# One written-out sequence for the heads of the mLSTM and differential attentions

## Chip, cores and metric

One core of one Trainium2 chip runs the whole program in a single launch. The metric is the device time of that launch in microseconds, the median of several runs.

## What is computed

The reference passes 256 tokens of width 1024 through a first block of two layers and a second block of two layers. Each layer of the first block is a mixer, an attention to a memory of 256 tokens, and a convolutional feed-forward part; the second block has a feed-forward part, a hybrid mixer, an attention to a second memory, and another feed-forward part. Two of the mixers hold an attention with *two* sets of scores for each of four heads, each head with values of width 128:

```python
# layer 0: mLSTM, forward and backward in time (bwd is the same on flipped inputs)
sc  = einsum('bhtd,bhsd->bhts', qc, kc) * exp(log_d - m_t)      # log_d from the gates, causal
h   = (sc @ v) / maximum(abs(sum(sc)), exp(-m_t))               # fwd + bwd are added
# layer 1: differential attention
p   = softmax(q1 @ k1.T + bias) - lam * softmax(q2 @ k2.T + bias)
out = p @ v
...
# everything around them is matrix products in float32
x = x + mixer(...) ; x = x + cross_attention(x, mem) ; x = x + conv_ffn(x)
```

## The kernel before, in words

**Products in float32.** Each float32 factor is kept as two parts of reduced precision (a rounded `hi` and the rest `lo`), and a product is three matmuls, x_hi·w_lo, x_lo·w_hi and x_hi·w_hi, summed in one PSUM bank (lines 882, 883 and 885). Weights arrive in chunks of 128x2048 numbers. A chunk's way is: a DMA by SyncE into one of three `raw` buffers (line 760), the rounded part by ScalarE (`whi`, line 1398), and the subtraction raw − whi either by VectorE as one instruction (`wlo`, line 1843) or by GpSimd as four (line 850). There are three buffers of `whi` and `wlo`, so rounding chunk c waits until TensorE has used chunk c − 3, and a new DMA waits until the chunk three before it has been subtracted. A list made while the program is built says which engine subtracts: chunks whose units are first used as fillers of an attention or heads stage go to GpSimd if that stage was built after `on_pool` was set (its field `late`).

**Units and fillers.** A unit is one accumulation of two 128x256 results, held in one of two banks; a bank is free again when its result has been copied out, by ScalarE for units called "plain" (line 1416), else by VectorE (lines 1861, 1870 and 1874). Attention and "heads" (normalisation) stages have small matmuls that wait for other engines, so units of later linear layers are put between them: `fill` is a table from a slot to (the unit up to which TensorE goes, the unit up to which the others copy out, and optionally how many chunks ahead they prepare). Slot "pre" lies at the barrier between two stages, where every engine drains and then waits for the two others. TensorE does the slot's units before that wait, ScalarE and VectorE do theirs behind it.

**The fillers here.** In the mLSTM stage: H0 and H1 (two half-length residual units of the output weights, from one chunk), then K0 to K3 (keys and values of the memory, one chunk each, behind a chunk that holds the memory's activations). H2 and H3, from one chunk, come in the heads stage behind it. In the differential stage: K3, then H0, H1, H2; H3 comes behind it.

**The two stages.** Both are built by `attention(...)` and carried out by three functions called `dual`, one in the program of each engine. One head i is:

- TensorE: `scores(i)` (line 1236, for the mLSTM also line 1249), `turn(i)` (four transposes, line 1260), `values(i)` (line 1269).
- VectorE: `front(i)` (biased scores and their extremes, line 2147, and 2305), `prob(i)` (for the mLSTM line 2323 on; scaling in lines 2334 and 2337), `output(i)` (line 2343).
- ScalarE: `front(i)` (exponentials, line 1710), `back(i)` (copies the transposed probabilities, line 1721).

The score banks of two heads exist, so `scores(i)` waits for `prob(i-2)`; the transposes share one bank, and so do the results of `values`. Before the change each engine ran a loop over i with a fixed distance `lag` of 2 between the first and the last step of a head:

```python
# TensorE                          # ScalarE                        # VectorE
scores(i)                          # empty_and_fill(st, i)          # empty(st, i); front(i)
fill(st, i)                        # front(i)                       # fill(st, i)
turn(i - lag)                      # back(i - lag)                  # prob(i - 1)
values(i - lag - 1)                # (tanh at i == 6)               # output(i - lag - 1)
```

`empty` copies out units up to the slot's second number, `split_upto(reach(st, slot))` prepares chunks. Each engine works through its program in order, so whatever stands in front of a step holds it up.

## Time and profile before

| | us |
|---|---|
| median of 3 runs | 2294.79 |
| lowest and highest | 2292.48, 2295.53 |
| the profiled execution's own time | 2294.97 |
| its span in the profile | 2293.2 |
| TensorE busy in it | 2203.7 (96%) |
| VectorE, ScalarE, GpSimd busy | 1504.9, 1108.0, 355.9 |
| chain that ended last, TensorE's share | 85% |
| the mLSTM stage in it | about 133 to 186 us |
| the differential stage in it | about 572 to 606 us |

The span is what the profiler saw from first to last instruction; the execution's own time is 1.8 us longer. Times in rows are counted from the span's start. A row of a timeline is the start, the time taken, engine, line, instruction, and in brackets how long the engine had been idle before it and what ended that idleness. `x4` says that four instructions are merged in the row.

### The profile page before, as it was taken

The numbers are of one execution on the slowest core, as the hardware profiler recorded it, in microseconds if no ns is written. First come the engines' busy times: TensorE is split into PE (matmuls) and PEld (weight loads), VectorE is DVE, ScalarE is ACT, GpSimd is POOL, SyncE is SP. The second block draws the span as 40 slices with busy tenths as digits, with TensorE's granted clock in tenths as the row PEclk, the third lists the DMA queues.
The fourth block names the chain that finished last, engine by engine and source line by source line (L and its number), as shares of the span: only waits on it lengthen the run. The fifth ranks groups of instructions, "written<-read, shape, count | busy, mean of one in ns | idle before, by whom it ended". The sixth has DMA issues, their size and how long they took to land.

```text
span 2293.2 us, 40427 instructions
## 1 busy us (share of the span) xinstructions
PE 2203.7 (96%) x17458; PEld 2112.2 (92%) x17458; DVE 1504.9 (66%) x2210; ACT 1108.0 (48%) x1335; POOL 355.9 (16%) x300
## 2 busy tenths in 40 slices
PE   8988999998799999999999999999999999999998
PEld 7777899997689999999988799999999998799998
DVE  6656787843578787567766657657656566657655
ACT  5345654544465445335646455335334456455333
POOL 2760000055000000000645120000000015320000
PEclk9989999999999999999999999999999999999999
DMA  8653355543245555546643354555555653355552
GB/s 280 181 165 111 111 188 198 176 158 117 92 131 168 200 174 189 189 166 184 195 143 104 124 182 163 195 176 184 184 184 167 175 166 105 117 171 169 185 184 92
DMA packets 316964, 375.13 MB, mean 164 GB/s; under 512 B 27255, under 2 KB 283011, under 8 KB 315635
## 3 DMA queue, kind: packets, MB, share of 16 engines
q1 hardware_dynamic: 311635, 354.88, 47.4%
q0 software_dynamic: 3424, 11.50, 1.8%
q10 hardware_dynamic: 1728, 6.17, 0.7%
q8 instruction: 138, 2.26, 0.4%
q14 instruction: 39, 0.32, 0.0%
HBM read 363.34 MB, written 9.18 MB: 162 GB/s over the span
## 4 chain that ended last, share of the span: by engine, by line
PE 85%; DVE 7%; ACT 3%; issue 2%; DMA 1%; SPq 1%; DVEq 0%; POOL 0%; ACTq 0%
PE banks L882 24%; PE banks L885 23%; PE banks L883 23%; PE banks L923 3%; PE banks L924 3%; PE banks L927 3%; DVE wlo L1843 2%; PE banks L1147 1%; DMA raw<-in_ev_w_in 1%; PE banks L1185 1%; ACT whi L1398 1%; PE banks L1171 1%; PE banks L1045 1%; SPq L760 1%; PE banks L892 0%
## 5 line engine op out<-in xcount | busy, mean ns | idle before, releaser
L882 PE MATMUL banks<-x_hi,wlo 128*128 128x256 f32 (+1 forms) x4344 | 1101.5, 286 | 18.2 <-DVE gt L1879 6.9
L883 PE MATMUL banks<-x_lo,whi 128*128 128x256 f32 (+1 forms) x4344 | 1092.3, 284 | 0.0
L1398 ACT ACTIVATE whi<-raw 128x2048 fp32r<-128x2048 f32 (+3 forms) x340 | 637.7, 1879 | 601.1 <-PE banks L885 551.8
L882 PEld LDWEIGHTS banks<-x_hi,wlo 128*128 128x128 f32 (+1 forms) x4344 | 838.4, 193 | 37.0 <-issue 19.8
L883 PEld LDWEIGHTS banks<-x_lo,whi 128*128 128x128 f32 (+1 forms) x4344 | 839.0, 193 | 0.0
L1843 DVE TENSOR_TENSOR wlo<-raw,whi 128x2048 fp32r<-128x2048 f32 (+4 forms) x290 | 652.3, 2260 | 120.6 <-ACT whi L1398 120.3
L885 PE MATMUL banks<-x_hi,whi 128*128 128x256 f32 x4344 | 687.9, 284 | 0.0
L885 PEld LDWEIGHTS banks<-x_hi,whi 128*128 128x128 f32 x4344 | 595.8, 193 | 3.2
L850 POOL TENSOR_TENSOR wlo<-raw,whi 128x512 fp32r<-128x512 f32 x192 | 251.7, 1347 | 1121.4 <-ACT whi L1398 1121.4
L923 PE MATMUL banks<-x_hi,wlo 128*128 128x256 f32 (+1 forms) x624 | 170.5, 305 | 13.9 <-DVE gt L1879 5.0
L924 PE MATMUL banks<-x_lo,whi 128*128 128x256 f32 (+1 forms) x624 | 163.9, 295 | 0.0
L923 PEld LDWEIGHTS banks<-x_hi,wlo 128*128 128x128 f32 (+1 forms) x624 | 127.6, 204 | 20.8 <-issue 6.1
L2409 DVE TENSOR_TENSOR wk<-banks,norm_scale 128x512 f32<-128x512 f32 x132 | 90.9, 689 | 74.2 <-PE banks L885 69.6
L924 PEld LDWEIGHTS banks<-x_lo,whi 128*128 128x128 f32 (+1 forms) x624 | 127.7, 205 | 0.4
L805 POOL TENSOR_SCALAR gt<-gt,cols 128x256 f32<-128x256 f32 x32 | 42.6, 1343 | 544.8 <-DVE gt L1921 544.8
L2448 DVE CAST x_hi<-wk 128x512 fp32r<-128x512 f32 x66 | 28.2, 427 | 131.6 <-PE banks L885 130.6
L2427 DVE SCALAR_TENSOR_TENSOR wk<-wk,cols 128x255 f32<-128x255 f32 x176 | 73.4, 480 | 39.4 <-ACT wk L1763 38.7
L882 PE MATMUL banks<-whi,x_lo 128*128 128x256 f32 (+3 forms) x400 | 96.7, 282 | 0.0
L883 PE MATMUL banks<-wlo,x_hi 128*128 128x256 f32 (+3 forms) x400 | 95.3, 279 | 0.0
L927 PE MATMUL banks<-x_hi,whi 128*128 128x256 f32 (+1 forms) x632 | 92.9, 285 | 0.0
L1763 ACT ACTIVATE wk<-wk,cols 128x256 f32<-128x256 f32 x88 | 45.7, 590 | 92.0 <-DVE wk L2409 92.0
L1447 ACT ACTIVATE x_hi<-xT,con,cols 128x256 fp32r<-128x256 f32 x112 | 60.9, 590 | 59.7 <-DVE xT L1874 49.8
(264 smaller groups left out, 1939.0 us busy)
## 6 DMA issues: line engine op xcount, KB each, us to landing
raw<-in_ffn_w_gu SPq DMA_DIRECT2D x88, 1024.0 KB, 5.1
raw<-in_ffn_w_down SPq DMA_DIRECT2D x66, 1024.0 KB, 5.2
raw<-in_ffn_w_up SPq DMA_DIRECT2D x44, 1024.0 KB, 5.1
raw<-in_w_in SPq DMA_DIRECT2D x38, 1024.0 KB, 5.2
raw<-in_ca_w_kv SPq DMA_DIRECT2D x16, 1024.0 KB, 5.3
raw<-in_od_w_in SPq DMA_DIRECT2D x12, 1024.0 KB, 5.3
raw<-in_ev_w_in SPq DMA_DIRECT2D x10, 1024.0 KB, 7.4
raw<-in_ca_w_q SPq DMA_DIRECT2D x8, 1024.0 KB, 5.1
```

The source lines that it names most:

```text
L850: m = eng.tensor_tensor(wlo[s][:, at:at + PIECE], full[:, at:at + PIECE], whi[s][:, at:at + PIECE].bitcast(F32), ALU.subtract)
L882: eng.matmul(out, a[1], b[0], start=first and i == 0, stop=False, skip_group_check=True)
L883: eng.matmul(out, a[0], b[1], start=False, stop=False, skip_group_check=True)
L885: m = eng.matmul(out, a[0], b[0], start=False, stop=last and i == len(operands) - 1, skip_group_check=True)
L923: eng.matmul(bank[:, o], a[1], b[0], start=i == 0 and k0 + k == 0, stop=False, skip_group_check=True)
L924: eng.matmul(bank[:, o], a[0], b[1], start=False, stop=False, skip_group_check=True)
L927: m = eng.matmul(bank[:, o], a[0], b[0], start=False, stop=k == n - 1, skip_group_check=True)
L1398: eng.activation(whi[s % SETS][:, 0:ch["n"]], raw[i % SLOTS][:, 0:ch["n"]], ACT.Copy).then_inc(S["weights_hi"], 1)
L1447: eng.activation(X[nm["buf"]][0][:, k, :], xT[:, k, :], ACT.Identity, scale=cols[:, nm["gain"] + k:nm["gain"] + k + 1], bias=C("zero")).th ...
L1843: eng.tensor_tensor(wlo[s][:, 0:n], full[:, 0:n], whi[s][:, 0:n].bitcast(F32), ALU.subtract).then_inc(S["weights_split"], 1)
L2409: return eng.tensor_tensor(wk[:, half, :].rearrange("p (n c) -> p n c", c=SEQ), bank[:, :].rearrange("p (n c) -> p n c", c=SEQ), norms, AL ...
L2427: m = eng.scalar_tensor_tensor(out=o, in0=wk[:, half, i * SEQ:(i + 1) * SEQ][:, src], scalar=cols[:, w:w + 1], in1=o, op0=ALU.mult, op1=AL ...
```

## The change

In both stages the loop over i gives way to a sequence written out step by step, in one agreed order for the three engines. Both first scores come ahead of all fillers. On TensorE `turn(i)` comes right behind `scores(i+2)`. ScalarE takes both first fronts before rounding further chunks, and no longer rounds two chunks ahead in a row before a front. VectorE takes `prob` ahead of chunk subtractions. In the differential stage slot 0 prepares one chunk ahead and no more.

In the mLSTM stage the chunk of K0 is now rounded at the barrier ("pre", 3 chunks ahead). `on_pool` is set after that stage instead of before it, so of this stage's chunks only K0's stays with GpSimd; the chunks of H0/H1, K1, K2 and K3 are subtracted by VectorE.

```diff
@@ even_mixer
-            on_pool[0] = True
+            chunks[units_of[K[0]]["chunk"]]["on_pool"] = True
             attention("mlstm", [...],
-                      fill={"pre": (M[7] + 1, M[7] + 1, 2), 0: (H[1] + 1, M[7] + 1, 2), 1: (K[1], K[0]), 2: (K[2], K[1]), 3: (K[3], K[2]), 4: (K[3] + 1, K[3])},
-                      tanh={6: M[7] + 1})
+                      fill={"pre": (M[7] + 1, M[7] + 1, 3), 0: (H[1] + 1, H[1], 3), 1: (K[1], K[0]), 2: (K[2], K[0]), 3: (K[3], K[2]), 4: (K[3] + 1, K[3])},
+                      tanh=M[7] + 1)
+            on_pool[0] = True
@@ odd_mixer
             attention("difference", [...],
-                      fill={0: (H[1], K[3]), 1: (H[2], H[1]), 2: (H[3], H[2])})
+                      fill={0: (H[1], K[3], 1), 1: (H[2], H[1]), 2: (H[3], H[2])})
@@ tensor, dual
-                for i in range(len(units) + lag + 1):
-                    if i < len(units):
-                        scores(i)
-                    fill(st, i)
-                    if 0 <= i - lag < len(units):
-                        turn(i - lag)
-                    if i - lag >= 1:
-                        values(i - lag - 1)
+                scores(0)
+                scores(1)
+                fill(st, 0)
+                if kind == "mlstm":
+                    fill(st, 1)
+                scores(2)
+                turn(0)
+                scores(3)
+                if kind == "mlstm":
+                    values(0)
+                    turn(1)
+                    fill(st, 2)
+                    values(1)
+                    turn(2)
+                    fill(st, 3)
+                    values(2)
+                    turn(3)
+                    fill(st, 4)
+                    values(3)
+                else:
+                    fill(st, 1)
+                    turn(1)
+                    values(0)
+                    fill(st, 2)
+                    values(1)
+                    turn(2)
+                    values(2)
+                    turn(3)
+                    values(3)
@@ scalar, dual
+                if kind == "mlstm":
+                    front(0)
+                    front(1)
+                    round_ahead(st, 0)
+                    evac_upto(st["fill"][1][0])
+                    round_ahead(st, 1)
+                    back(0)
+                    back(1)
+                    front(2)
+                    front(3)
+                    empty(st, 3)
+                    round_ahead(st, 2)
+                    back(2)
+                    empty(st, 4)
+                    round_ahead(st, 3)
+                    back(3)
+                    round_ahead(st, 4)
+                    flush(st["tanh"])
+                else:
+                    empty(st, 0)
+                    round_ahead(st, 0)
+                    front(0)
+                    front(1)
+                    empty(st, 1)
+                    round_ahead(st, 1)
+                    back(0)
+                    front(2)
+                    front(3)
+                    back(1)
+                    round_ahead(st, 2)
+                    back(2)
+                    back(3)
@@ vector, dual
+                front(0)
+                front(1)
+                if kind == "mlstm":
+                    empty(st, 0)
+                    prob(0)
+                    empty(st, 1)
+                    prob(1)
+                    split_upto(reach(st, 0))
+                    front(2)
+                    front(3)
+                    split_upto(reach(st, 1))
+                    output(0)
+                    prob(2)
+                    prob(3)
+                    output(1)
+                    split_upto(reach(st, 2))
+                    output(2)
+                    split_upto(reach(st, 3))
+                    output(3)
+                    split_upto(reach(st, 4))
+                else:
+                    prob(0)
+                    prob(1)
+                    empty(st, 1)
+                    front(2)
+                    front(3)
+                    prob(2)
+                    output(0)
+                    prob(3)
+                    empty(st, 2)
+                    output(1)
+                    split_upto(reach(st, 1))
+                    output(2)
+                    split_upto(reach(st, 2))
+                    output(3)
```

**How the instructions move.** ScalarE in the mLSTM stage. `x_hi<-raw` is the memory's chunk, `whi<-raw` a rounded weight chunk, `wk<-wk,stat` the exponentials of a front, `ft<-banks` the copy-out of K0, `wk<-banks` a `back`. Before:

```order
L1391 ACTIVATE x_hi<-raw 128x2048
L1398 ACTIVATE whi<-raw 128x2048
L1710 ACTIVATE wk<-wk,stat 128x256 x4
L1713 ACTIVATE stat<-stat 128x4
L1398 ACTIVATE whi<-raw 128x2048 x2
L1710 ACTIVATE wk<-wk,stat 128x256 x4
L1713 ACTIVATE stat<-stat 128x4
L1416 ACTIVATE ft<-banks 128x512
L1398 ACTIVATE whi<-raw 128x2048
L1710 ACTIVATE wk<-wk,stat 128x256 x4
```

With the change:

```order
L1413 ACTIVATE x_hi<-raw 128x2048
L1420 ACTIVATE whi<-raw 128x2048
L1734 ACTIVATE wk<-wk,stat 128x256 x4
L1737 ACTIVATE stat<-stat 128x4
L1734 ACTIVATE wk<-wk,stat 128x256 x4
L1737 ACTIVATE stat<-stat 128x4
L1420 ACTIVATE whi<-raw 128x2048
L1438 ACTIVATE ft<-banks 128x512
L1420 ACTIVATE whi<-raw 128x2048
L1745 ACTIVATE wk<-banks 128x512 x2
```

The exponentials of head 1 no longer have two roundings in front of them; the two first `back` steps stand together behind the chunk of K2.

TensorE in the mLSTM stage, behind K0 (`banks<-x_hi,whi` is the end of its product). Before, this place holds one pair of scores and then the next filler:

```order
L885 MATMUL banks<-x_hi,whi 128x256 x8
L1236 MATMUL banks<-ft 128x256 x2
L1249 MATMUL banks<-gate_rows_parts,pick 128x512
L882 MATMUL banks<-x_hi,wlo 128x256
L883 MATMUL banks<-x_lo,whi 128x256
```

With the change two heads' scores, two turns and one `values` stand there:

```order
L886 MATMUL banks<-x_hi,whi 128x256 x8
L1237 MATMUL banks<-ft 128x256 x2
L1250 MATMUL banks<-gate_rows_parts,pick 128x512
L1261 MATMUL banks<-con,wk 128x128 x4
L1237 MATMUL banks<-ft 128x256 x2
L1250 MATMUL banks<-gate_rows_parts,pick 128x512
L1270 MATMUL banks<-wk,vt 128x256 x2
L1261 MATMUL banks<-con,wk 128x128 x4
L883 MATMUL banks<-x_hi,wlo 128x256
```

ScalarE in the differential stage (`vt<-banks` copies out K2, then K3). Before:

```order
L1416 ACTIVATE vt<-banks 128x2x256
L1398 ACTIVATE whi<-raw 128x2048 x2
L1710 ACTIVATE wk,stat<-wk,stat 128x256 x4
L1416 ACTIVATE vt<-banks 128x2x256
L1710 ACTIVATE wk,stat<-wk,stat 128x256 x4
L1398 ACTIVATE whi<-raw 128x2048
```

With the change:

```order
L1438 ACTIVATE vt<-banks 128x2x256
L1420 ACTIVATE whi<-raw 128x2048
L1734 ACTIVATE wk,stat<-wk,stat 128x256 x8
L1438 ACTIVATE vt<-banks 128x2x256
L1420 ACTIVATE whi<-raw 128x2048
L1745 ACTIVATE wk<-banks 128x512
```

One rounding of the two stands behind both first fronts and behind the copy-out of K3.

## Rows read from the trace of the kernel before

**Rows 1.** The page: busy time of each engine over the whole span.

```profile
PE 2203.7 (96%) x17458; PEld 2112.2 (92%) x17458; DVE 1504.9 (66%) x2210; ACT 1108.0 (48%) x1335; POOL 355.9 (16%) x300
```

**Rows 2.** The stretches' busy PE, PEld, DVE, ACT, POOL; PEclk, DMA share, GB/s.

```profile
133.00:186.00 53.00, 45.48 (x292) 40.09 (x292) 37.17 (x105) 26.07 (x37) 25.82 (x20) 0.87 0.44 150
572.00:606.00 34.00, 26.89 (x186) 23.03 (x184) 19.89 (x63) 16.97 (x41) 6.01 (x5) 0.95 0.39 129
```

**Rows 3.** Waits between 132 and 190 us: engine, line <- awaited: total us, times, longest.

```profile
PE banks L1236 <- DVE wk L2337: 5.8, 1, 5.8
PE banks L1260 <- DVE wk L2337: 0.9, 1, 0.9
PE banks L1269 <- DVE ft L2343: 0.6, 1, 0.6
```

**Rows 4.** VectorE's timeline, first and last rows of `prob(0)`, then of `prob(1)`.

```profile
147.16 0.41 DVE L2323 CUSTOM_DVE_ANT_0 wk<-banks,wk 128x256 f32<-128x256 f32 x1
153.66 2.77 DVE L2337 SCALAR_TENSOR_TENSOR wk<-wk,stat 128x256 f32<-128x256 f32 x2
...
160.90 0.42 DVE L2323 CUSTOM_DVE_ANT_0 wk<-banks,wk 128x256 f32<-128x256 f32 x1
163.65 0.88 DVE L2337 SCALAR_TENSOR_TENSOR wk<-wk,stat 128x256 f32<-128x256 f32 x2
```

**Rows 5.** GpSimd's timeline, 132 to 172 us.

```profile
136.77 5.44 POOL L850 TENSOR_TENSOR wlo<-raw,whi 128x512 fp32r<-128x512 f32 x4 [6.66 <-ACT whi L1398]
143.44 15.33 POOL L850 TENSOR_TENSOR wlo<-raw,whi 128x512 fp32r<-128x512 f32 x12 [1.23 <-ACT whi L1398]
```

**Rows 6.** TensorE around its longest wait, ScalarE behind K0, the stretch after the wait.

```profile
143.32 1.03 PE L1236 MATMUL banks<-ft 128*128 128x256 f32 x4
...
150.76 0.60 ACT L1416 ACTIVATE ft<-banks 128x512 f32<-128x512 f32 x1 [1.68 <-PE banks L885]
...
156.49 2.07 PE L1236 MATMUL banks<-ft 128*128 128x256 f32 x4 [5.77 <-DVE wk L2337]
...
156.00:160.00 4.00, 3.51 (x8) 2.25 (x9) 1.11 (x4) 0.00 (x0) 2.77 (x3) 0.50 0.51 194
```

**Rows 7.** Timelines at the first stage's end: VectorE, ScalarE, TensorE.

```profile
176.71 2.29 DVE L1843 TENSOR_TENSOR wlo<-raw,whi 128x2048 fp32r<-128x2048 f32 x1 [0.92 <-ACT whi L1398]
...
186.60 1.91 ACT L1398 ACTIVATE whi<-raw 128x2048 fp32r<-128x2048 f32 x1 [0.24 <-DVEq L1817]
...
189.45 0.81 PE L1045 MATMUL banks<-wk,con 128*8 128x256 f32 x3 [0.24 <-ACT wk L1578]
```

**Rows 8.** Waits between 572 and 610 us.

```profile
ACT whi L1398 <- PE banks L885: 4.9, 1, 4.9
PE banks L1260 <- ACT wk L1721: 2.8, 1, 2.8
PE banks L1236 <- DVE wk L2337: 2.8, 2, 2.2
PE banks L882 <- ACT vt L1416: 0.7, 1, 0.7
```

**Rows 9.** The second stage: ScalarE's first exponentials, TensorE's tail, the clock there.

```profile
581.43 0.49 ACT L1710 ACTIVATE wk<-wk,stat 128x256 f32<-128x256 f32 x1
...
596.20 1.03 PE L1269 MATMUL banks<-wk,vt 128*128 128x256 f32 x4
...
600.51 1.92 PE L1269 MATMUL banks<-wk,vt 128*128 128x256 f32 x4
...
605.16 1.10 PE L1269 MATMUL banks<-wk,vt 128*128 128x256 f32 x4 [0.61 <-DVE ft L2343]
...
600.00:604.00 4.00, 3.97 (x15) 3.30 (x16) 1.85 (x5) 1.19 (x2) 0.00 (x0) 0.57 0.00 0
```

**Rows 10.** Timelines behind the second stage: ScalarE, TensorE.

```profile
606.86 1.34 ACT L1578 ACTIVATE wk<-ft 128x256 f32<-128x256 f32 x4 [2.95 <-DVEq L1817]
...
609.55 1.68 PE L1045 MATMUL banks<-wk,con 128*8 128x256 f32 x7
```

More of the change, by code:

```diff
@@ L464, in attention @@
             alone = all(len(un["heads"]) == 1 for un in units) if not dual else False
-            stage("attention", att=kind, units=units, alone=alone, u0=number("att", len(units)), bufs=2, lag=2,
+            stage("attention", att=kind, units=units, alone=alone, u0=number("att", len(units)), bufs=2,
                   sc=[banks[i] for i in (0, 1, 6, 7)] if dual else bank_pairs[0], pt=[banks[2]] if dual else bank_pairs[1],
@@ L1230, in dual @@
             def dual(st):
-                units, kind, bufs, lag = st["units"], st["att"], st["bufs"], st["lag"]
+                units, kind, bufs = st["units"], st["att"], st["bufs"]
                 sc, pt, ob = st["sc"], st["pt"], st["ob"]
@@ L1422, in fill, with empty, round_ahead @@
                     evac_upto(st["fill"][slot][1])
-            def empty_and_fill(st, slot):
-                if slot in st["fill"]:
-                    evac_upto(st["fill"][slot][1])
-                    split_upto(reach(st, slot))
+            def empty(st, slot):
+                evac_upto(st["fill"][slot][1])
+            def round_ahead(st, slot):
+                split_upto(reach(st, slot))
             gated = [0]
@@ L1701, in dual @@
             def dual(st):
-                units, kind, bufs, lag, pt = st["units"], st["att"], st["bufs"], st["lag"], st["pt"]
+                units, kind, bufs, pt = st["units"], st["att"], st["bufs"], st["pt"]
                 def front(i):
@@ L1721, in back @@
                     eng.activation(probsT_flat[b], pt[0], ACT.Copy).then_inc(S["att_pts"], 1)
-                for i in range(len(units) + lag + 1):
-                    if i < len(units) + lag:
-                        empty_and_fill(st, i)
-                    if i < len(units):
-                        front(i)
-                    if lag <= i < len(units) + lag:
-                        back(i - lag)
-                    if i in st.get("tanh", {}):
-                        flush(st["tanh"][i])
+                if kind == "mlstm":
[30 more added lines that the diff above has]
+                    back(3)
             def index(st):
@@ L2282, in dual @@
             def dual(st):
-                units, kind, bufs, lag = st["units"], st["att"], st["bufs"], st["lag"]
+                units, kind, bufs = st["units"], st["att"], st["bufs"]
                 sc, ob = st["sc"], st["ob"]
@@ L2343, in output @@
                     eng.tensor_copy(units[i]["dst"], ob[0][:, 0:SEQ]).then_inc(S["att_done"], 1)
-                for i in range(len(units) + lag + 1):
-                    empty(st, i)
-                    if i < len(units):
-                        front(i)
-                    fill(st, i)
-                    if 1 <= i <= len(units):
-                        prob(i - 1)
-                    if i - lag >= 1:
-                        output(i - lag - 1)
+                front(0)
[33 more added lines that the diff above has]
+                    output(3)
             def index(st):
```

## The prediction

> **What bounds the kernel now.** The page comes first: TensorE is busy 96% of the span [rows 1]. So only time in which TensorE stands idle, or runs at its lower clock, can be won by moving instructions. The busy times by stretch then say where that is: in the mLSTM stage TensorE is busy 45.5 of 53 us at a mean granted clock of 0.87, in the differential stage 26.9 of 34 us at 0.95, while no other engine is full in either; VectorE is nearest with 37.2 of 53 us [rows 2]. Outside the two stages the change moves only one subtraction.
>
> Third, the waits. In the first stage TensorE waits once for 5.8 us, for line 2337, the end of `prob(0)`, then 0.9 and 0.6 us at the end [rows 3]. Why is `prob(0)` late? VectorE's timeline has it from 147.16 to 156.43, 9.3 us, and `prob(1)` from 160.90 to 164.53, 3.6 us, for the same instructions; line 2337, for one, takes 1.4 us a piece in the one and 0.44 in the other [rows 4]. GpSimd subtracts weight pieces without a gap from 143.4 to 158.8, over the whole of `prob(0)` and not over `prob(1)` [rows 5]. So GpSimd's work makes it 5.6 us longer, and besides it stands behind `front(1)`. After the wait the granted clock is 0.50 from 156 to 160 (1.2 GHz), and four score matmuls take 2.07 us instead of 1.03 [rows 6].
>
> In the second stage ScalarE stands still 4.9 us in front of a rounding whose buffer TensorE still uses, with the exponentials of head 0 queued behind it. TensorE then waits 0.7 us for a copy-out, 2.8 us in two pieces for `prob`, and 2.8 us for a `back` [rows 8]. It waits 0.6 us more for an `output`, and from 600 to 604 it has a clock of 0.57: a `values` step takes 1.92 us instead of 1.03 [rows 9].
>
> **The change, part by part.** No matmul is added or removed. I count TensorE's lost time in each stage, and then what stays of it.
>
> *mLSTM, what goes.* `prob(0)` is issued behind both fronts and the copy-out of H0, but with H0, H1 and K0 of TensorE's work in front of the `scores(2)` that need it: all that work ends at 150.76 now, where ScalarE copies K0 out [rows 6], and no later in the new order, since it is the same work. Before, `scores(1)` started at 143.32 behind H0 and H1 [rows 6]; now they are done ahead, so the fronts and H0's copy-out are over by some 142. GpSimd then has only K0's four pieces, 5.4 us from 136.8 [rows 5], done by 142.2, just as `prob(0)` starts. At the price of `prob(1)`, 3.6 us [rows 4], it ends near 146, and `prob(1)` near 150. The wait of 5.8 us goes. With it goes the slow clock: 3.5 us busy at half clock [rows 2, 6] cost 1.75 us. The two waits at the end, 0.9 and 0.6 us, stand between `turn` and `values` steps with no filler; now K3 lies between `values(2)` with `turn(3)` and `values(3)`, so they go. Sum: 5.8 + 0.9 + 0.6 + 1.75 = 9.05 us.
>
> *mLSTM, what comes.* VectorE takes over the subtractions of K1, K2 and K3, 2.29 us each by [rows 7]; that of H0/H1 falls into the attention before, where VectorE is waiting. Its busy time goes from 37.2 by +6.9, and by −5.6 for the shorter `prob(0)`: about as before, so it is no bound over the stage. Late next is each chunk: K1's ends near 152.5 and is needed near 155.5, K2's has some 4 us of margin, K3's some 2. Cost nothing; if those margins fail, TensorE waits the difference. The last subtraction (the first chunk of the linear layer to come) moves from the middle of the stage behind `output(3)`, in front of the barrier: +2.29 us for ScalarE, which waits there for VectorE and whose rounding at 186.60 and squares lead to TensorE's sums at 189.45 [rows 7]. TensorE has H2 as cover, about 3 us, and before it had only 0.24 us of wait left there, so I count the 2.29 in full. `values(0)` needs `back(0)`, which stands behind the copy-out of K0 and a rounding (0.6 + 1.9 us behind K0's end [rows 6, 7]), against scores, turn and scores on TensorE, 3.3 us: a close race. I take 0.7 us for it and the longer queues; bounds are 0 and the 1.9 us of a rounding [rows 7]. Net: 9.05 − 2.29 − 0.7 = 6.0 us.
>
> *Differential stage.* ScalarE rounds one chunk, then does both fronts, so the exponentials no longer stand behind a wait of 4.9 us and a rounding of 1.9; they start near 575 instead of 581.43 [rows 8, 9]. K3 and H0 cover both `prob` steps, which need no unit of their stage. The waits of 0.7, 2.8 and 2.8 us [rows 8] and of 0.6 us [rows 9] go, 6.9 in all, and the slow clock, (1 − 0.57) x 3.97 = 1.7 us [rows 9]. Left is the end: behind H2 there are no fillers, and the chain `turn`, `back`, `values` stays for heads 2 and 3, each with about 0.8 us in which TensorE waits for the copy. 8.6 − 1.6 = 7.0; I take 0.4 off for hops between engines: 6.6 us. Behind the stage ScalarE's squares start at 606.86, TensorE's sums at 609.55 without a wait [rows 10], so a stage that ends earlier moves them as a whole; VectorE's two subtractions, now at the end, finish about when TensorE does.
>
> *Other edits.* The earlier rounding of K0's chunk changes nothing on ScalarE: it was already the next instruction there. The subtraction of H0/H1 on VectorE frees a `raw` buffer earlier. Those of the following linear layer free theirs some 8 to 14 us later in the differential stage; the DMAs behind them have the whole heads stage as cover, more than 20 us. I count zero; uncovered, a transfer would cost up to what is gained.
>
> **Sum.** 6.0 + 6.6 = 12.6 us. 2294.97 − 12.6 = 2282.4 for the profiled execution; the median of the runs is 0.2 us lower: 2282.2. The bounds: 0.7 + 0.4 back and the split hidden gives 2278.5; with both stages at half, 2288.5.
>
> The Trainium skill (SBUF — State Buffer, "Who interferes with whom") says that a VectorE instruction with two SBUF inputs, or in a 2-port mode, is fully blocked while a GpSimd instruction holds their common port, and that a VectorE instruction with at most one SBUF input is not. The slow line 2337 has two SBUF inputs and is the longer one beside GpSimd [rows 4], so the trace agrees. By that rule alone each moved subtraction would itself be open to such a block, by up to one GpSimd piece; the sum would change by about 1.3 us, since only K0's four pieces still run in the stage's first part.
>
> **Rivals.**
> 1. *The slow clock stays in the differential tail.* TensorE still has thin work there, heads 2 and 3 without fillers. For it: the clock fell behind a stretch of that kind at 600. Against: two waits of 0.8 us instead of 2.2 and 2.8. Price 1.7 us: 2283.9. The Trainium skill (TensorE: Matmul & The Clock Gate, "What's actually happening") says that the activity of the engine decides its clock; by that rule either outcome is possible here, and the price is that of rows 9. Chance 0.15.
> 2. *Only one stage gains in full.* In the differential tail VectorE's `output(1)`, a 2.3 us subtraction and `output(2)` are in one queue; if `values(3)` waits for `output(2)` behind that subtraction, and TensorE's tail keeps its length, that stage gives 2 us: 2286.8. Chance 0.12.
> 3. *The stall only moves.* `prob(0)` now stands behind the copy-out of H0, and each stage's end behind VectorE's subtractions; or a late DMA of the next layer takes the gain back. Then 2294.8. Against it: `prob(0)` has some 8 us up to K0's end for its 3.6. Chance 0.08.
> 4. *VectorE becomes the bound, and it is slower.* If its `prob` steps stayed at the 9.3 us that `prob(0)` has beside GpSimd, for all four heads, VectorE would need 37.2 + 6.9 + 3 x 5.6 = 61 us in a stage that lasts 53. It decides from the point where VectorE's need passes 53 us, that is from two contended heads on. It gives +8 us, +3.5 for two slow-clock spells as in [rows 6], +3.5 for first scores and last values outside VectorE's part, −6.6 from the other stage: 2303. Against: 12 of the 16 GpSimd pieces in [rows 5] are gone. Chance 0.04.
>
> **Numbers.** My forecast has 0.61: 2282.2, its own range 2278.5 to 2286. A measurement here can tell 0.2%, 4.6 us, so faster means below 2290.2. Forecast and rivals 1 and 2 are faster: 0.61 + 0.15 + 0.12 = 0.88, of which I move 0.02 to "same" for a sum that is too high throughout: 0.86. Same: 0.08 + 0.02 = 0.10. Slower: 0.04. Range: 2278.5 to 2289.5, which leaves out rivals 3 and 4 and the tails.
>
> **What would show it.** In the profile of the changed kernel: no wait of TensorE for line 2384 (the old 2337) above 1 us in the mLSTM stage; `prob(0)` in 3.6 to 4.5 us; GpSimd with four pieces there before 145; a granted clock of 1.0 from about 140 on; TensorE's sums behind the stage near 183.5 instead of 189.5. In the differential stage: exponentials of head 0 near 569 (575 less the 6 us already won), sums near 597 instead of 609.55. POOL busy falls by 16 pieces, about 20 us, and that by itself wins nothing. The prediction is wrong if TensorE waits for a `wlo` of VectorE inside the stages, if VectorE is busy without a gap in the first, or if the gain up to 190 or 610 us is lost again in the next attention.

## The result, and the profile after

| | before | changed |
|---|---|---|
| median of six runs each, us | 2294.76 | 2283.11 |
| lowest and highest | 2292.48, 2295.53 | 2277.11, 2285.82 |
| the profiled execution's own time | 2294.97 | 2277.11 |
| ratio, with its 95% interval | | 0.9948 [0.9934, 0.9962] |

The profiled execution of the changed kernel is its fastest run, 6 us below the median. So the two traces differ by more than the medians do, and the first question is where. The starts of four places, taken from TensorE's timelines (the ends are the spans'):

| us | before | changed | difference |
|---|---|---|---|
| first scores of the mLSTM stage | 133.05 | 131.95 | -1.1 |
| sums behind that stage | 189.45 | 181.02 | -8.4 |
| first scores of the differential stage | 572.43 | 564.08 | -8.4 |
| sums behind that stage | 609.55 | 593.60 | -16.0 |
| end of the span | 2293.2 | 2275.3 | -17.9 |

The mLSTM stage gives 7.3 us (56.40 to 49.07), the differential stage 7.6 us (37.12 to 29.52). Between the two stages nothing is given back in this profile. 1.1 us ahead of the first stage and 1.9 us behind the second lie in code that the change does not touch; the experiments below tell more of both.

The page of the changed kernel answers [rows 1]: TensorE and GpSimd are less busy, VectorE a little more.

```profile
PE 2198.8 (97%) x17458; PEld 2108.5 (93%) x17458; DVE 1507.4 (66%) x2214; ACT 1107.6 (49%) x1335; POOL 336.0 (15%) x284
...
PE 89%; DVE 6%; ACT 3%; issue 1%; DVEq 0%; DMA 0%; ACTq 0%
```

The second line is the chain that ended last: TensorE has 89% of it, where it had 85%. GpSimd lost 19.9 us and 16 pieces; VectorE gained only 2.5 us, since its `prob(0)` alone is 5.6 us shorter.

The waits between 131 and 183 us, of TensorE and what it meets at the stage's end, answer [rows 3]:

```profile
DVE ft L2390 <- PE banks L1270: 7.9, 2, 6.6
...
ACT whi L1420 <- DVEq L1864: 3.5, 1, 3.5
...
PE banks L1046 <- ACT wk L1602: 2.3, 1, 2.3
...
PE banks L1237 <- DVEq L1864: 1.1, 1, 1.1
```

TensorE's 5.8, 0.9 and 0.6 us are gone. What is left is the 1.1 us at the barrier in front of the stage, which was there before, and a new one of 2.3 us for the squares behind the stage. VectorE's timeline shows `prob(0)` and `prob(1)`, first and last rows, then the first chunk's subtraction; it answers [rows 4]:

```profile
141.76 0.42 DVE L2370 CUSTOM_DVE_ANT_0 wk<-banks,wk 128x256 f32<-128x256 f32 x1
...
144.51 0.88 DVE L2384 SCALAR_TENSOR_TENSOR wk<-wk,stat 128x256 f32<-128x256 f32 x2
...
145.91 0.41 DVE L2370 CUSTOM_DVE_ANT_0 wk<-banks,wk 128x256 f32<-128x256 f32 x1
...
148.66 0.88 DVE L2384 SCALAR_TENSOR_TENSOR wk<-wk,stat 128x256 f32<-128x256 f32 x2
149.47 2.28 DVE L1890 TENSOR_TENSOR wlo<-raw,whi 128x2048 fp32r<-128x2048 f32 x1
```

`prob(0)` takes 3.6 us, from 141.76 to 145.39, where it took 9.3 us; `scores(2)` needs it only at 149.59. GpSimd's timeline, which answers [rows 5], has K0's four pieces and then nothing up to H2's chunk:

```profile
135.68 5.42 POOL L851 TENSOR_TENSOR wlo<-raw,whi 128x512 fp32r<-128x512 f32 x4 [10.12 <-ACT whi L1420]
169.97 5.05 POOL L851 TENSOR_TENSOR wlo<-raw,whi 128x512 fp32r<-128x512 f32 x4 [28.87 <-ACT whi L1420]
```

The busy times by stretch: the first stage from first scores to sums, the 33 us in which VectorE has no gap, the part behind 139 us, and two windows of 6 us [rows 2, 6]:

```profile
131.95:181.02 49.07, 46.54 (x316) 41.38 (x317) 36.13 (x109) 28.78 (x41) 10.46 (x8) 0.93 0.43 138
...
134.00:167.00 33.00, 33.00 (x226) 29.43 (x227) 32.14 (x105) 16.76 (x29) 5.42 (x4) 0.93 0.39 128
...
139.00:181.00 42.00, 39.49 (x300) 36.84 (x299) 31.08 (x96) 24.76 (x39) 7.15 (x6) 1.00 0.46 150
150.00:156.00 6.00, 6.00 (x36) 4.62 (x36) 5.93 (x20) 4.22 (x7) 0.00 (x0) 1.00 0.43 160
156.00:162.00 6.00, 6.00 (x47) 5.54 (x47) 5.83 (x24) 4.22 (x10) 0.00 (x0) 1.00 0.57 189
```

From 139 us on the granted clock is 1.00 (2.4 GHz); the 0.50 behind the old stall does not come back. And VectorE, which had 37 of the stage's 53 us before, is all but full for two thirds of the stage: 32.1 of the 33 us from 134 to 167, and 11.8 of the 12 from 150 to 162. At the stage's end three timelines (VectorE, ScalarE, TensorE) show the new wait; they answer [rows 7]:

```profile
175.42 0.42 DVE L2390 COPY ft<-banks 128x256 f32<-128x256 f32 x1 [6.64 <-PE banks L1270]
175.76 2.28 DVE L1890 TENSOR_TENSOR wlo<-raw,whi 128x2048 fp32r<-128x2048 f32 x1
...
178.18 1.91 ACT L1420 ACTIVATE whi<-raw 128x2048 fp32r<-128x2048 f32 x1 [3.53 <-DVEq L1864]
...
181.02 1.24 PE L1046 MATMUL banks<-wk,con 128*8 128x256 f32 x5 [2.27 <-ACT wk L1602]
```

VectorE stands idle for 6.64 us in front of `output(3)` and then subtracts for 2.28 us; ScalarE waits at the barrier for that, rounds, makes the squares, and TensorE stands 2.27 us for them. In the differential stage the waits answer [rows 8], the timeline of TensorE's tail and the clock of the same stretch [rows 9], ScalarE's squares and TensorE's sums [rows 10]:

```profile
PE banks L1270 <- ACT wk L1745: 1.4, 2, 0.7
```

```profile
586.92 1.13 PE L1270 MATMUL banks<-wk,vt 128*128 128x256 f32 x4 [0.69 <-ACT wk L1745]
587.89 0.60 PE L1261 MATMUL banks<-con,wk 128*128 128x128 f32 x4
589.18 1.13 PE L1270 MATMUL banks<-wk,vt 128*128 128x256 f32 x4 [0.69 <-ACT wk L1745]
...
591.47 1.34 ACT L1602 ACTIVATE wk<-ft 128x256 f32<-128x256 f32 x4 [2.34 <-DVEq L1864]
...
593.60 0.60 PE L1046 MATMUL banks<-wk,con 128*8 128x256 f32 x2
```

```profile
584.00:588.00 4.00, 3.31 (x21) 2.77 (x21) 3.21 (x5) 0.60 (x1) 0.00 (x0) 1.00 0.00 0
588.00:592.00 4.00, 3.06 (x21) 2.40 (x20) 3.77 (x5) 1.13 (x3) 0.00 (x0) 1.00 0.55 168
```

Two waits of 0.69 us are left, and the clock stays at 1.00. The same tail before, by its windows, shows what lay in front of the drop there: TensorE had been busy 3.0 of 8 us.

```profile
592.00:596.00 4.00, 1.80 (x15) 1.20 (x14) 2.64 (x8) 1.06 (x4) 0.00 (x0) 1.00 0.48 150
596.00:600.00 4.00, 1.23 (x8) 0.77 (x6) 3.83 (x18) 2.56 (x9) 0.00 (x0) 1.00 0.29 112
```

### The profile page after: what moved, and what is told of

It reads as the page before. It is cut to its first block, busy times and chain, and to the rows that moved or that the text cites. A ratio compares the mean times of both kernels' runs of the same rounds, so it can differ in the third digit from the quotient of the medians.

```text
span 2275.3 us, 40415 instructions
## 1 busy us (share of the span) xinstructions
PE 2198.8 (97%) x17458; PEld 2108.5 (93%) x17458; DVE 1507.4 (66%) x2214; ACT 1107.6 (49%) x1335; POOL 336.0 (15%) x284
## 4 chain that ended last, share of the span: by engine, by line
PE 89%; DVE 6%; ACT 3%; issue 1%; DVEq 0%; DMA 0%; ACTq 0%
PE banks L883 24%; PE banks L886 24%; PE banks L884 24%; PE banks L924 3%; PE banks L925 3%; PE banks L928 3%; DVE wlo L1890 2%; PE banks L1148 2%; PE banks L1186 1%; PE banks L1172 1%; PE banks L1046 1%; PE banks L893 0%; PE banks L1237 0%; ACT whi L1420 0%; DVE ft L2145 0%
## 5 line engine op out<-in xcount | busy, mean ns | idle before, releaser
L883 PE MATMUL banks<-x_hi,wlo 128*128 128x256 f32 (+1 forms) x4344 | 1100.0, 286 | 13.4 <-DVE gt L1926 5.4
L1890 DVE TENSOR_TENSOR wlo<-raw,whi 128x2048 fp32r<-128x2048 f32 (+2 forms) x294 | 661.6, 2261 | 114.7 <-ACT whi L1420 114.3
L851 POOL TENSOR_TENSOR wlo<-raw,whi 128x512 fp32r<-128x512 f32 x176 | 231.4, 1349 | 1130.2 <-ACT whi L1420 1130.2
```

Source lines behind the costliest of these rows:

```text
L851: m = eng.tensor_tensor(wlo[s][:, at:at + PIECE], full[:, at:at + PIECE], whi[s][:, at:at + PIECE].bitcast(F32), ALU.subtract)
L883: eng.matmul(out, a[1], b[0], start=first and i == 0, stop=False, skip_group_check=True)
L1890: eng.tensor_tensor(wlo[s][:, 0:n], full[:, 0:n], whi[s][:, 0:n].bitcast(F32), ALU.subtract).then_inc(S["weights_split"], 1)
```

## The experiments

Twelve runs followed, two of them of the changed kernel again, in three sets, each set beside runs of the kernel before (medians 2294.67, 2294.02 and 2295.13 us). For each kernel there are two measures: the median of its runs, and, from the one profile of each, the length of each stage from the first scores to the sums behind it. The second turned out to be the sharper one, for a reason that the first set shows.

**The changed kernel again, twice.**

> The changed kernel once more, unedited, for a second profile. My steps: 2282 to 2284 as a median; in the profile the shift against before is about -8 us over the mLSTM stage and about -6.3 us over the differential stage, as in the first profile (190.9 against 182.9 less 1.1 us gained ahead of it; 611.4 against 595.4). The 1.1 us ahead of the stage and the 2.5 us near 1240 to 1330 us of the first profile lie in unedited code: if they are chance, this profile lacks one or both of them, and its span is 2278 to 2284; if they are caused by the change, they stand in it again.

> The changed kernel unedited, a third time, beside the versions that are to beat it. Both stages' times as in its two profiles (first scores to sums 49.0 and 29.5 us); the median between 2276 and 2284, depending on the clock and the start of unedited stages.

The changed kernel came out at 2276.60 us (ratio 0.9918 [0.9902, 0.9934]), 5 us under what was expected, and 2278.90 us (0.9923 [0.9902, 0.9944]), after 2283.11 in the first set. Its stages hardly vary: 49.07, 48.96 and 48.95 us, and 29.52, 29.54 and 29.53 us. What varies lies elsewhere. In the second profile the lead over the kernel before is 15.1 us behind the differential stage and 15.2 us at the end of the span, so the 2.5 us that the first profile gained between 1236 and 1333 us were chance. The clock differs there too: in the 10 us around 1285 the granted clock is 0.71 in the kernel before and in the second profile, 0.83 in the first. In the third profile 1.7 us of the gain are lost between the two stages, with no new wait of TensorE: from 230 to 240 us the clock is 0.75 there and 0.95 in the first. Over all fourteen profiles this unedited stretch between the stages lasts 381.7 to 385.9 us.

The first scores of the mLSTM stage start, over all fourteen profiles, between 128.75 and 141.18 us, though no edit touches the code ahead of them, and the granted clock there is 0.50 in some and 1.00 in others, of the same kernel too. The first rows of the stage in the first profile and in the next of the changed kernel, six us each:

```profile
132.00:138.00 6.00, 6.00 (x13) 3.46 (x14) 4.07 (x9) 3.60 (x2) 2.32 (x2) 0.50 0.11 20
```

```profile
132.50:138.50 6.00, 6.00 (x36) 4.75 (x37) 4.06 (x9) 3.62 (x2) 2.30 (x2) 1.00 0.10 31
```

With the whole clock TensorE gets through 36 matmuls where it got through 13, and yet the stage is no shorter. The waits of TensorE in that second profile, 132 to 182 us, say why:

```profile
PE banks L1046 <- ACT wk L1602: 2.3, 1, 2.3
...
PE banks L1261 <- DVE wk L2384: 1.8, 1, 1.8
...
PE banks L883 <- DVE xT L1921: 1.0, 1, 1.0
```

It waits 1.0 us for the copy-out of H0, which VectorE does behind both fronts, and 1.8 us at `turn(2)` for `prob(2)`. So VectorE's chain now sets the stage's length. Five profiles of this stage agree: TensorE's two waits for VectorE are 2.8 us in all in the two that start at the whole clock (`again`, `only_mlstm`), 1.4 us in one that starts low for some 4 us (`diff_lookahead`), and nothing in the two that start low for 6 us or more, and the length is 48.95 to 49.07 us in all five. In the old order the low clock at the start did cost time: 56.40 us with it, 54.81 without.

**One stage at a time.** The old loop (in all three `dual`) and the old table are put back for one of the two stages; here for the differential one:

```diff
-                      fill={0: (H[1], K[3], 1), 1: (H[2], H[1]), 2: (H[3], H[2])})
+                      fill={0: (H[1], K[3]), 1: (H[2], H[1]), 2: (H[3], H[2])})
...
+                if kind != "difference":
...
+                else:
+                    for i in range(len(units) + lag + 1):
```

> The changed kernel with the differential stage's old loop and old filler table. My steps: the two stages are independent, so the gain is the mLSTM stage's alone, 6 (forecast) to 8 us (first profile): 2286.5 to 2289. Rival (only one stage gains in full, the mLSTM's): 2283 to 2285, as the full change.

> The changed kernel with the mLSTM stage's old loop, table and division between VectorE and GpSimd. My steps: 6 to 6.6 us gained, 2288 to 2289; together with the kernel that has the mLSTM stage alone the gains add up to that of the full change within 1.5 us. Rival (the differential stage gives only 2 us): 2292.5 to 2293.

| | mLSTM stage, us | differential stage, us | median, us | ratio |
|---|---|---|---|---|
| before | 56.40 | 37.12 | 2294.67 | |
| mLSTM alone changed | 48.97 | 37.12 | 2287.70 | 0.9974 [0.9963, 0.9986] |
| differential alone changed | 54.81 | 29.53 | 2283.95 | 0.9955 [0.9939, 0.9972] |
| both (again) | 48.96 | 29.54 | 2276.60 | 0.9918 [0.9902, 0.9934] |

Each stage keeps its length whatever the other one has, and the medians add up: they fall by 7.0, 10.7 and, together, 18.1 us. The kernel with the differential stage alone came out 4 us faster than expected. Its stage gives 7.6 us by its length; the other 3 of the 10.7 us are not the edit's, and up to 1.6 of them may be the whole clock at the start of its old mLSTM stage.

**Order or division of the subtractions?** In the mLSTM stage the change does two things: it writes the order anew, and it takes three chunks from GpSimd. The division alone (which engine subtracts) was undone in the changed kernel, and made alone in the kernel before by the opposite edit:

```diff
-            chunks[units_of[K[0]]["chunk"]]["on_pool"] = True
+            on_pool[0] = True
...
-            on_pool[0] = True
```

> The changed order in both stages, but the chunks of H0/H1, K1, K2 and K3 stay with GpSimd. My steps: prob(0) now has 8 us of cover, so most of the wait stays away even with GpSimd beside it; prob(1) and prob(2) grow from 3.6 to 6 to 9 us, and scores(3) or turn(2) waits 1 to 4 us for them: 2284 to 2287. Rival (contention for the port is all there is, the order is worth nothing in the mLSTM stage): the stage's whole gain goes, 2289 to 2291. Rival (the order is all there is): 2282 to 2284.

> The kernel before, with its old loops, and only the division of the mLSTM stage's subtractions changed as in the change (K0 with GpSimd, H0/H1, K1, K2, K3 with VectorE). My steps: prob(0) shrinks from 9.3 to 3.6 us, but the old loop puts the subtractions of K1 and K2, 4.6 us, ahead of it, so it ends at about the same time; TensorE still waits 4 to 6 us for line 2337, and the time from the stage's first scores to the sums behind it stays 54 to 57 us (56.4 before): 2293 to 2296. Rival (GpSimd's contention is the cause of the stall): the wait falls to under 1 us, the time to under 51 us: 2288 to 2290.

| mLSTM stage, us (median of the runs) | three chunks on GpSimd | on VectorE |
|---|---|---|
| old order | 54.81, 56.40 (2294.67) | 52.66 (2292.36) |
| new order | 49.89 (2281.33) | 49.0 (2276.60) |

The order, with its table, is worth 3.7 us with the chunks on VectorE and 4.9 to 6.5 us with them on GpSimd (49.89 has the low clock at its start, like 56.40). The division is worth 2.2 us in the old order (both with the whole clock at the start) and 0.9 us in the new. Both results lie outside what was expected. With the chunks on GpSimd the new order was to have waits of 1 to 4 us, and has two of 0.4 and 0.2 us: `prob(0)` and `prob(1)` take 4.7 and 4.9 us beside GpSimd, and TensorE's work in front covers that. The old order with the chunks on VectorE was to take 54 us or more, or under 51, and takes 52.66. The medians of the new order (2281.33 and 2276.60) have overlapping intervals, so the 0.9 us rest on the stage's length alone.

Why does the old order not gain more from an undisturbed `prob(0)`? VectorE's timeline in that kernel, 142 to 152 us:

```profile
143.65 4.49 DVE L1844 TENSOR_TENSOR wlo<-raw,whi 128x2048 fp32r<-128x2048 f32 x2
148.06 0.42 DVE L2324 CUSTOM_DVE_ANT_0 wk<-banks,wk 128x256 f32<-128x256 f32 x1
...
150.80 0.88 DVE L2338 SCALAR_TENSOR_TENSOR wk<-wk,stat 128x256 f32<-128x256 f32 x2
```

`prob(0)` takes 3.6 us there too, but it starts at 148.06, behind two subtractions that now are VectorE's own, and TensorE's wait for it is still 3.8 us, against 5.6 us in the old order with GpSimd from the same clock. What GpSimd did beside `prob(0)`, VectorE does in front of it. The larger part of the fix is the place of `prob` in the sequence; the division helps in either order, and less in the new one.

**One subtraction in front of `prob(0)`.** The next edit tests VectorE's place in the sequence directly, in the changed kernel:

```diff
+                    split_upto(reach(st, 0))
                     prob(0)
                     empty(st, 1)
                     prob(1)
-                    split_upto(reach(st, 0))
```

> The changed kernel with one line moved: in the mLSTM stage VectorE subtracts K1's chunk ahead of prob(0) instead of behind prob(1). My steps (a probability step must stand ahead of subtractions): prob(0) then waits for ScalarE's rounding and the 2.3 us of the subtraction, ends 2.5 to 5 us later, and scores(2) waits 1.5 to 4 us for it; the stage grows from 49.0 to 50.5 to 52 us. Rival (TensorE's cover of H0, H1 and K0 alone does it, VectorE's order is worth nothing): no wait at scores(2), 49 us.

The stage takes 53.91 us instead of 48.95 (the changed kernel in the same set, clock 0.50 at the start of both), and the median is 2283.11 against 2278.90. That is more than the 50.5 to 52 us expected: one moved line costs 5.0 us. VectorE waits 3.03 us for the chunk's rounding, which ScalarE has behind the exponentials of head 1, then subtracts for 2.29 us, and `prob(0)` starts at 148.52, over 5 us later. From TensorE's timeline, and the windows from 154 on:

```profile
152.21 1.13 PE L1237 MATMUL banks<-ft 128*128 128x256 f32 x4 [1.01 <-DVE wk L2384]
...
156.35 1.30 PE L1237 MATMUL banks<-ft 128*128 128x256 f32 x4 [2.00 <-DVE wk L2384]
...
158.31 2.07 PE L1270 MATMUL banks<-wk,vt 128*128 128x256 f32 x4
```

```profile
154.00:157.00 3.00, 1.00 (x7) 0.71 (x6) 2.83 (x14) 0.60 (x1) 0.00 (x0) 1.00 0.00 0
157.00:160.00 3.00, 3.00 (x8) 1.77 (x7) 2.38 (x14) 0.00 (x0) 0.00 (x0) 0.53 0.00 0
```

3.0 us of it are two waits of TensorE, and the clock falls behind them to 0.53: a `values` step takes 2.07 us instead of 1.03. By the windows that clock costs (1 - 0.53) x 3 = 1.4 us up to 160, and some 0.3 us more up to 162 (granted clock 0.85), which is 1.7 of the remaining 2.0 us. Here 3.0 us of waits cost 5.0 us.

**Look-ahead in the old loop of the differential stage.** Is it the third number in the table, one chunk ahead instead of two, that frees the exponentials? The mLSTM stage is the changed one here, the differential stage has the old loop:

```diff
-                      fill={0: (H[1], K[3]), 1: (H[2], H[1]), 2: (H[3], H[2])})
+                      fill={0: (H[1], K[3], 1), 1: (H[2], H[1]), 2: (H[3], H[2])})
```

> The kernel with the new mLSTM stage alone, and in the differential stage's old loop just the new number in its filler table: one chunk ahead in slot 0, not two. My steps: ScalarE's stall of 4.9 us in front of the first exponentials and TensorE's 0.7 us behind it go, the tail stays: first scores to sums 35.5 to 36.5 us, against 37.1 in the old stage and 29.5 in the new one; 1 us faster than the new mLSTM stage alone. Rival (the stall of ScalarE is the root of all waits of that stage): 31 us or less, 6 us faster.

The stage takes 39.44 us, 2.3 us more than with the old table (37.12), and both expectations missed it; the median is 2287.13, that of the kernel with the old table 2287.70, no difference that the runs can tell. In VectorE's timeline a subtraction now stands between the first fronts and `prob(0)`, whose last part is the last row:

```profile
574.70 2.29 DVE L1919 TENSOR_TENSOR wlo<-raw,whi 128x2048 fp32r<-128x2048 f32 x1
...
578.03 0.88 DVE L2413 SCALAR_TENSOR_TENSOR wk<-wk,stat 128x256 f32<-128x256 f32 x2
```

TensorE's `scores(2)` waits 2.6 us for it. So in the old sequence the new number gains nothing, and a subtraction in front of `prob(0)` costs time in this stage too. Which other reordering of this stage brings the 7.6 us no run takes apart.

**The subtraction at the mLSTM stage's end.** The new wait of 2.27 us behind that stage should go if the last subtraction is made while VectorE is idle for 6.6 us in front of `output(3)`:

```diff
-                    output(3)
                     split_upto(reach(st, 4))
+                    output(3)
```

> The changed kernel, with VectorE's last subtraction of the mLSTM stage in front of output(3) instead of behind it. VectorE is idle 6.6 us in that place. If the subtraction behind output(3) costs its 2.3 us at the barrier, as I counted, first scores to sums goes from 49.0 to 47.0 us, TensorE's wait of 2.3 us there disappears, and the median falls by 2 us against the changed kernel's (2276.6 and 2283.1 in two sets). Rival (the 2.3 us are hidden by H2 and the work behind the barrier): no change.

> As the kernel with the early subtraction, and K2's subtraction goes to GpSimd, which is idle there. In the second profile of the changed kernel, with a full clock from the start, turn(2) waits 1.8 us for prob(2), which stands behind K2's subtraction. If VectorE is the bound there, that wait goes with a full clock at the start (sums 45.2 to 45.5 us after the first scores) and nothing changes with a slow start (47.0). Rival (GpSimd's contention gives it back): prob(2) or a front grows by 1.3 us or more for each piece it meets, and the stage stays at 47.

The second of these also gives K2's chunk to GpSimd. The stage takes 48.08 and 47.65 us (47.0 were expected, or less), medians 2276.60 and 2277.06. The wait for the squares is gone in both, but the first wins only 0.9 us: TensorE waits 1.69 us for H2's pieces from GpSimd instead. TensorE's row, then VectorE's and GpSimd's ahead of it, in the first of the two:

```profile
186.20 0.39 PE L883 MATMUL banks<-x_hi,wlo 128*128 128x256 f32 x1 [1.69 <-POOL wlo L851]
...
181.33 2.46 DVE L1890 TENSOR_TENSOR wlo<-raw,whi 128x2048 fp32r<-128x2048 f32 x1 [3.43 <-ACT whi L1420]
...
179.09 7.05 POOL L851 TENSOR_TENSOR wlo<-raw,whi 128x512 fp32r<-128x512 f32 x4 [28.73 <-ACT whi L1420]
```

GpSimd's four pieces take 7.05 us beside that subtraction instead of 5.05. The next kernel gives H2's chunk to VectorE as well, by setting `on_pool` behind the heads stage, and the one after it gives K2's to GpSimd besides:

```diff
+            chunks[units_of[K[2]]["chunk"]]["on_pool"] = True
...
-            on_pool[0] = True
...
+            on_pool[0] = True
```

> The early subtraction alone met a new wait: H2 waited 1.7 us for GpSimd's four pieces, which VectorE's early subtraction now ran beside. Here the chunk of H2/H3 goes to VectorE too, which is idle then. If that wait is what gave the gain back: no wait at H2, first scores to sums 46.5 to 47.2 us (49.0 in the changed kernel, 48.1 with the early subtraction alone), the median 2 us under the changed kernel's in this set. Rival (ScalarE's roundings are next, and give it back again): 48 us.

> As early_both, with K2's subtraction on GpSimd. That move shortened the stage by 0.4 us on top of the early subtraction (48.1 to 47.7). If it adds up: 46 to 46.8 us, and a median of 2.5 us under the changed kernel's in this set.

| third set | mLSTM stage, us | median, us | ratio |
|---|---|---|---|
| the changed kernel | 48.95 | 2278.90 | 0.9923 [0.9902, 0.9944] |
| both edits | 46.77 | 2275.65 | 0.9908 [0.9887, 0.9929] |
| and K2 on GpSimd | 46.34 | 2273.46 | 0.9900 [0.9879, 0.9921] |

Now the wait's worth is won: 48.95 falls to 46.77, as expected, and in both kernels TensorE's sums follow H2 without a wait. In the second:

```profile
174.27 0.36 PE L884 MATMUL banks<-x_hi,wlo 128*128 128x256 f32 x1 [0.26 <-issue]
...
177.46 3.61 PE L1047 MATMUL banks<-wk,con 128*8 128x256 f32 x16
```

K2's chunk on GpSimd takes 0.4 us off the stage, here and in the pair before (48.08 to 47.65, both from a low clock); the wait at `turn(2)` falls with it, from 1.4 to 1.0 us in the pair before, whose starts have the same clock. The last kernel beats the kernel before and the changed one by its median; its interval against that of the changed kernel overlaps, so the proof is the stage's length and not the median.

## Why the prediction was right, point by point

The forecast of 2282.2 us, 12.6 us less than before, stands beside 2283.1 in the first set; the other two sets gave 2276.6 and 2278.9. The closeness of the first is partly luck. The stages themselves gave 5.8 to 7.4 us and 7.6 us, 13.4 to 15.0 in all, so the sum was 1 to 2.4 us too small, and the rest of the difference between sets lies outside the stages. The lower bound was added up wrongly: its terms (0.7, 0.4 and 2.29) give 2278.8, not 2278.5.

**The mLSTM stage, forecast 6.0 us.**
- *The wait of 5.8 us goes.* Right, and at the forecast times: `prob(0)` from 141.8, 3.6 us long. The reason was only half right. I put the length of `prob(0)` down to GpSimd, which is so, and treated its place in the queue as an aside ("besides it stands behind `front(1)`"). The runs put it the other way round: the order is worth 3.7 us or more, the division 0.9 us in the new order and 2.2 us in the old.
- *The slow clock of 1.75 us goes.* Right: 1.00 from 139 us on. In the experiment that brings back 3.0 us of waits it comes back and costs about 1.7 us.
- *The waits of 0.9 and 0.6 us go.* Right.
- *The last subtraction costs 2.29 us in full.* Right: a wait of 2.27 us, where 0.24 us stood before. Moved ahead alone the subtraction gave back only 0.9 us, as H2's pieces came next.
- *`back(0)` costs 0.7 us.* Wrong size: `values(0)` has no wait in any profile of the changed kernel. The term was 0, the bound that the text gave.
- *VectorE "is no bound over the stage", and the margins "cost nothing".* This is the step that failed. It held in the first profile, where TensorE started at half clock and came late, though VectorE ran without a gap from 134 to 167 us, which the forecast had named as a sign of being wrong. In the second, with the whole clock, TensorE waits 1.0 and 1.8 us for VectorE, and the mark "no wait for line 2384 above 1 us" is broken. The stage mean (37 of 53 us) hid that stretch: 32.1 of 33 us busy. The total did not suffer, since the old order lost more than VectorE's bound takes.
- Together: the terms that hold are 9.05 less 2.03 (2.27 without the 0.24 of before), 7.0 us. Measured are 7.3 us from slow start to slow start. From fast start to fast start it is 5.8 us (54.81 to 48.97), since VectorE's bound then holds TensorE back.

**The differential stage, forecast 6.6 us, measured 7.6.** All waits of [rows 8] and the 0.6 us of [rows 9] are gone. Each of the two new waits is 0.69 us, not 0.8. The slow clock is gone. Those terms give 6.9 + 1.7 - 1.4 = 7.2 us, and the 0.4 us that I took off "for hops between engines" had no ground; 0.4 us are missing on the other side, and no run says where they come from. The exponentials of head 0 came 9.0 us behind the stage's first scores and now come 2.8 us behind them (566.89, forecast near 569).

**The other edits** were put at zero, and the first profile shows no price: the 8.4 us won by the end of the first stage are all there at the first scores of the second. Of the 16.0 us won by the end of the second, some 15.3 remain 30 us later and stay constant up to 1,230 us. No DMA took the gain back there.

**The rivals.** The slow clock in the differential tail (rival 1) did not come: 1.00 from 580 to 592, with TensorE busy 6.4 of the last 8 us instead of 3.0. I had cited the Trainium skill (TensorE: Matmul & The Clock Gate, "What's actually happening") for an outcome open either way; the rows of this tail agree that the clock follows activity. The last section has a place where they do not settle it. `values(3)` never waited for `output(2)` (rival 2). The stall did not move (rival 3): no new wait of TensorE took the gain between or behind the stages, and the 1.7 us lost there in the third profile were lost at a lower clock. VectorE did not make the kernel slower (rival 4), though it was the right engine to watch. The rule of the Trainium skill on the shared port (SBUF — State Buffer, "Who interferes with whom") would have put 1.3 us, by the forecast's estimate, on the moved subtractions. Beside no GpSimd work they took 2.28 us as before, so this cost nothing; where the two did meet, in the early-subtraction kernel, the VectorE one took 2.46 us and GpSimd lost 2.0 us.

**What stays open.** Why the same code before the mLSTM stage ends anywhere from 128.75 to 141.18 us, what makes the clock differ at the same place of the same program, and why the changed kernel's median was 2283.1 in one set and 2276.6 in another, no run here explains. The kernel before moved by only 1.1 us between the sets. And only VectorE's order was tested by itself; what the new orders of TensorE and ScalarE are worth alone is not shown.

## What to carry to other kernels

Where several engines work through their programs in order and wait for each other, look first at the step that the bounding engine needs next, and at what stands in front of it on the helper: one subtraction of 2.3 us, with the wait for its input, in front of `prob(0)` cost 5.0 us here, as waits and as the slower clock behind them. Moving that work to another engine gained less (0.9 to 2.2 us) than moving it behind the step (3.7 us or more). A busy share taken over a whole stage hides 33 us in which the helper engine is full. When a program has chance shifts of several us, compare the length of the edited stage in the traces, at the same clock at its start, rather than the medians.

## What the runs showed of the hardware that was not expected

- *The clock at one place of one program is not fixed.* At the first scores of the mLSTM stage the granted clock is 0.50 (1.2 GHz) in the first and third profile of the changed kernel and 1.00 (2.4 GHz) in the second. In the 10 us ahead of it TensorE is busy the same in all fourteen profiles (2.0, 2.0, 2.0, 0.9 and 0.9 us of each 2), at a clock of 0.93 or more; then five start at 1.00, five at 0.50, and four at some 0.57 for the first 4 us. In the old order the low start costs 1.6 us (56.40 against 54.81), in the new nothing.
- *Beside GpSimd a tiny VectorE instruction loses as much as a longer one.* In the kernel before, of `prob(0)` beside GpSimd (rows of VectorE's timeline):

```profile
147.51 0.41 DVE L2323 CUSTOM_DVE_ANT_0 wk<-banks,wk 128x256 f32<-128x256 f32 x1
...
148.65 1.10 DVE L2326 SCALAR_TENSOR_TENSOR stat<-stat 128x4 f32<-128x4 f32 x1
149.79 1.22 DVE L2329 TENSOR_TENSOR stat<-stat 128x4 f32<-128x4 f32 x1
151.03 0.18 DVE L2331 RECIPROCAL stat<-stat 128x4 f32<-128x4 f32 x1
151.25 2.38 DVE L2334 TENSOR_SCALAR wk<-wk,stat 128x256 f32<-128x256 f32 x2
```

Two of four elements a partition take 1.10 and 1.22 us where they take 0.16 in the changed kernel, so each loses about 1 us; the two of 128x256 in the last row lose 0.9 us each (1.19 instead of 0.31). One GpSimd piece takes 1.3 us. The instruction that reads a PSUM bank keeps its 0.41 us, and so does the reciprocal its 0.18. In these runs a chain of small steps was worse to have beside GpSimd than one long subtraction, which lost 0.17 us while GpSimd lost 2.0.
